# A diffusion mixer layer: recurrence gates as 64x64 fp32 quarter products instead of split 128x128 products

## Reference

```python
def lru_coeffs(xc, wa, ba, wx, bx, lam):
    xh = xc.reshape(B_, N, LRU_HEADS, LRU_HD)                # 8 heads of 64 channels
    r = sigmoid(einsum('bnhi,hij->bnhj', xh, wa).reshape(B_, N, W_LRU) + ba)
    i = sigmoid(einsum('bnhi,hij->bnhj', xh, wx).reshape(B_, N, W_LRU) + bx)
    log_a = (-LRU_C * r) * softplus(-lam)
    a = exp(log_a)
    b = sqrt(-expm1(2.0 * log_a)) * (i * xc)
    return a, b                                              # h_t = a_t * h_(t-1) + b_t, forwards and backwards
```

## Time and profile before

| what | value |
|---|---|
| median of 3 runs | 792.26 us (788.52 to 792.53) |
| the profiled execution | 792.91 us, span 790.7 us |
| mean granted TensorE clock | 0.971 of full speed |
| busy PE / PEld / DVE / ACT / POOL | 739.8 / 602.7 / 526.6 / 449.5 / 272.5 us |
| the projection's and output's matmuls (lines 1544 to 1546) in the chain that ended last | 57% of the span |

### The profile page before, as it was taken

How to read it: one execution, slowest core, us unless ns; L and a number is a source line. 1 busy time by engine, 2 the same in 40 slices (tenths; PEclk the granted TensorE clock), 3 DMA queues, 4 the chain that set the end, 5 groups by cost and what they waited for, 6 DMA issues and landing times.

```text
span 790.7 us, 9934 instructions
## 1 busy us (share of the span) xinstructions
PE 739.8 (94%) x3468; PEld 602.7 (76%) x3468; DVE 526.6 (67%) x811; ACT 449.5 (57%) x743; POOL 272.5 (34%) x321
## 2 busy tenths in 40 slices
PE   3886989999999999999998999899999999999997
PEld 1574767888888887888887877677787888888885
DVE  4377653757998798887995754776646665666522
ACT  4266643699786986787884982234535133534311
POOL 0122335243534274234423345233211134353421
PEclk9796989999999999999999999899999999999999
DMA  8997003334365355345444043254458667968531
GB/s 360 369 325 225 27 28 96 105 97 117 115 182 151 86 157 176 112 141 162 146 130 137 34 127 135 82 160 134 116 194 315 223 205 244 302 202 293 181 116 72
DMA packets 89218, 130.11 MB, mean 165 GB/s; under 512 B 22768, under 2 KB 54128, under 8 KB 87632
## 3 DMA queue, kind: packets, MB, share of 16 engines
q1 hardware_dynamic: 84800, 115.44, 45.1%
q0 software_dynamic: 4368, 14.03, 6.4%
HBM read 91.17 MB, written 38.27 MB: 164 GB/s over the span
## 4 chain that ended last, share of the span: by engine, by line
PE 59%; DVE 14%; issue 7%; ACT 7%; DMA 7%; POOL 4%; SPq 1%; DVEq 0%; ACTq 0%; POOLq 0%
PE bank L1544 19%; PE bank L1546 19%; PE bank L1545 19%; DMA wm<-in_w_mod 3%; DMA pv<-scratch_u 1%; DVE xg L1186 1%; DVE Qb L1301 1%; DVE xc L1129 1%; ACT fbuf L895 1%; DVE spl L1348 1%; POOL xTh L609 1%; ACT bank L878 1%; DVE xTl L1194 1%; DVE Ib L1291 1%; DVE gacc L1129 1%
## 5 line engine op out<-in xcount | busy, mean ns | idle before, releaser
L1544 PE MATMUL bank<-xTh,wh 128*128 128x512 f32 (+1 forms) x592 | 238.2, 402 | 7.2 <-DVE xTl L1194 4.4
L1546 PE MATMUL bank<-xTh,wl 128*128 128x512 f32 (+1 forms) x592 | 231.9, 392 | 0.0
L1545 PE MATMUL bank<-xTl,wh 128*128 128x512 f32 x576 | 227.2, 395 | 0.0
L1544 PEld LDWEIGHTS bank<-xTh,wh 128*128 128x128 f32 x592 | 113.8, 192 | 32.8 <-DVE xTl L1194 6.4
L1546 PEld LDWEIGHTS bank<-xTh,wl 128*128 128x128 f32 x592 | 113.3, 191 | 23.7
L1545 PEld LDWEIGHTS bank<-xTl,wh 128*128 128x128 f32 x576 | 110.2, 191 | 22.6 <-issue 1.2
L1544 PE MATMUL bank<-xTh 128*128 128x512 f32 (+1 forms) x272 | 104.2, 383 | 1.3 <-issue 0.8
L1546 PE MATMUL bank<-xTh,xTl 128*128 128x512 f32 x256 | 99.6, 389 | 0.0
L1545 PE MATMUL bank<-xTl,xTh 128*128 128x512 f32 x256 | 99.6, 389 | 0.0
L911 ACT ACTIVATE ustage<-bank 128x512 f32<-128x512 f32 x56 | 33.1, 592 | 93.0 <-PE bank L1546 76.3
L609 POOL TENSOR_SCALAR sph<-xc 128x512 fp32r<-128x512 f32 (+1 forms) x36 | 27.1, 769 | 121.1 <-PE bank L1546 68.4
(11 more groups left out here) (192 smaller groups left out, 1413.0 us busy)
## 6 DMA issues: line engine op xcount, KB each, us to landing
scratch_u<-ustage SPq DMA_DIRECT2D x72, 256.0 KB, 3.3
wraw<-in_w_in SPq DMA_DIRECT2D x18, 512.0 KB, 4.6
wm<-in_w_mod SPq DMA_DIRECT2D x8, 1024.0 KB, 14.4
xg<-in_x SPq DMA_DIRECT2D x16, 512.0 KB, 9.0
yb<-scratch_y SPq DMA_DIRECT2D x32, 256.0 KB, 3.6
gb<-scratch_u SPq DMA_DIRECT2D x32, 256.0 KB, 5.1
xres<-in_x SPq DMA_DIRECT2D x16, 512.0 KB, 4.7
out<-tout SPq DMA_DIRECT2D x15, 512.0 KB, 3.0
```

The source lines that it names most:

```text
L1544: mm(out, wh_, xh_, start=first, stop=False)
L1545: mm(out, wh_, xl_, start=False, stop=False)
L1546: return mm(out, wl_, xh_, start=False, stop=last)
```

## The change

The gates become plain fp32 matmuls on the raw operands. Each of the four 64x64 blocks of a direction is a matmul of its own on a quarter of the array: input rows 0-63 or 64-127, output partitions 0-63 or 64-127. The recurrence gate `gr` uses the two diagonal quarters, the input gate `gi_` the two crossed ones, so the halves of `gi_` come out exchanged, and ACT takes them over crosswise with two sigmoids of 64 partitions for each direction. The splits of `xc` and of the gate weights go, with `sph`, `spl`, `gwh`, `gwl`, their zeroing and their semaphores; `gwr` gets two buffers. The sigmoid of `gr` goes to a new SBUF buffer `rb`, which holds the Tanh too. PE waits for the convolved pieces themselves and for all six sigmoids of the step before. The high parts of the projection weights 5 to 15 and of all conv weights move from ACT to POOL: those that stood behind the sigmoids now stand ahead of `gated_input(q)`, the others ahead of `add_y(q)`. On DVE `conv(here + 4)` moves from behind the scans of s = 0 to behind `one_minus_a2` of s = 1. The buffers behind keep their addresses.

```diff
@@ SBUF
-        sph = a3.take("sph", [P, 2, CH], f32r)
-        spl = a3.take("spl", [P, 2, CH], f32r)
...
-        gwh = a3.take("gwh", [P, 4, P], f32r)
-        gwl = a3.take("gwl", [P, 4, P], f32r)
-        gwr = a3.take("gwr", [P, 4, 64])
+        gwr = a3.take("gwr", [P, 2, 4, 64])
+        rb = a3.take("rb", [P, 2, CH])
+        a3.off += 4 * (2 * CH + 2 * 4 * P - 4 * 64)
@@ helpers
+        ON_POOL = [w for w in range(5, len(W_JOBS)) if w_split_at(w) <= GATES_AFTER[-1]]
@@ gpsimd
-            g.memset(gwh[:].bitcast(f32), 0.0).then_inc(s_gz, 1)
-            g.memset(gwl[:].bitcast(f32), 0.0).then_inc(s_gz, 1)
...
             def load_gate_w(t):
-                if t:
-                    pool.wait_ge(s_gwl, 2 * t)
-                g.dma_start(gwr[:], gate_w[t]).then_inc(s_gw, 16)
+                if t >= 2:
+                    pool.wait_ge(s_pg, (NCH + 1) * (t - 1))
+                g.dma_start(gwr[:, t % 2], gate_w[t]).then_inc(s_gw[t % 2], 16)
...
-            def gate_w_hi(t):
...
-            def split(q):
...
                 for d, c in enumerate((f, b)):
-                    pool.wait_ge(s_sig, 4 * q + d + 3)
+                    pool.wait_ge(s_sig, 6 * q + 2 * d + 4)
...
+            def w_hi(w):
+                pool.wait_ge(s_wr[w % 2], 16 * (w // 2))
+                pool.wait_ge(s_pu, w_slot_free(w))
+                round_hi(W_JOBS[w][1][0], w_raw(w)).then_inc(s_whp, 1)
+
+            def conv_w_hi(j):
+                pool.wait_ge(s_cwr[j % 2], 16 * (j // 2 + 1))
+                if j >= 2:
+                    pool.wait_ge(s_pu, N_CU + CONV_AT[j - 2] + 1)
+                round_hi(cwh[:, j % 2], cwraw[:, j % 2]).then_inc(s_cwhi, 1)
+
+            done_w, done_cw = 5, 0
+
+            def weights_hi(upto):
+
+                nonlocal done_w, done_cw
+                while done_w - 5 < len(ON_POOL) and w_split_at(done_w) <= upto:
+                    w_hi(done_w)
+                    done_w += 1
+                while done_cw < N_CONV and CONV_AT[done_cw] - 4 <= upto:
+                    conv_w_hi(done_cw)
+                    done_cw += 1
...
-            gate_w_hi(0)
-            split(0)
...
-                if s == NCH and more:
-                    gate_w_hi(t + 1)
                 if s == 0:
                     load_v(here + 4)
-                if q + 1 < STEPS:
-                    split(q + 1)
...
+                if GATES_AFTER[q] + 1 in WEIGHTS_BEHIND_GATES:
+                    weights_hi(GATES_AFTER[q] + 1)
                 gated_input(q)
...
                 for j in convs_in_step(q, 4):
                     conv_z_hi(j)
+                weights_hi(min(STEP_END[q], GATES_AFTER[-1]))
                 add_y(q)
@@ scalar, sigmoids
                 for d in range(2):
-                    r = gr[d][:, 0:n]
-                    a.activation(r, r, ACT.Sigmoid, bias=par_col("lru_ba", 4 * d + t)).then_inc(s_sig, 1)
+                    a.activation(rb[:, d, 0:n], gr[d][:, 0:n], ACT.Sigmoid,
+                                 bias=par_col("lru_ba", 4 * d + t)).then_inc(s_sig, 1)
                 for d in range(2):
                     if q:
                         act.wait_ge(s_st, 2 * (q - 1) + d + 1)
-                    a.activation(Ib[:, d, 0:n], gi_[d][:, 0:n], ACT.Sigmoid,
-                                 bias=par_col("lru_bx", 4 * d + t)).then_inc(s_sig, 1)
+                    for h, other in ((slice(0, 64), slice(64, 128)), (slice(64, 128), slice(0, 64))):
+                        a.activation(Ib[h, d, 0:n], gi_[d][other, 0:n], ACT.Sigmoid,
+                                     bias=par_col("lru_bx", 4 * d + t)[h]).then_inc(s_sig, 1)
@@ scalar, decays
-                    r = gr[d][:, 0:n]
+                    r = rb[:, d, 0:n]
@@ scalar, the loop over the steps
-                if GATES_AFTER[q] + 1 in WEIGHTS_BEHIND_GATES:
-                    weights_side(GATES_AFTER[q] + 1)
@@ vector, one_minus_a2
-                    stt(Qb[:, d, 0:n], Qb[:, d, 0:n], 1.0, gr[d][:, 0:n], ALU.add, ALU.mult).then_inc(s_m2, 1)
+                    stt(Qb[:, d, 0:n], Qb[:, d, 0:n], 1.0, rb[:, d, 0:n], ALU.add, ALU.mult).then_inc(s_m2, 1)
@@ vector, the loop over the steps
-                if s == NCH and t + 1 < N_LRU:
-                    gate_w_lo(t + 1)
...
                 one_minus_a2(q)
-                if q + 1 < STEPS:
-                    split_lo(q + 1)
+                if s == 1:
+                    conv(here + 4)
...
                 if s == 0:
                     conv(here + 3)
-                    conv(here + 4)
@@ tensor, gates
                 if s == 0:
-                    pe.wait_ge(s_gwl, 2 * t + 2)
-                pe.wait_ge(s_sl, splits_before(q + 1))
+                    pe.wait_ge(s_gw[t % 2], 16 * (t // 2 + 1))
+                pe.wait_ge(s_cv, (NCH + 1) * t + LAST_PIECE[s] + 1)
                 if q:
-                    pe.wait_ge(s_sig, 4 * q)
-                    pe.wait_ge(s_m2, 2 * q)
-                for m in range(4):
-                    d = 0 if s == 0 else m // 2
-                    b = gi_[m // 2] if m % 2 else gr[m // 2]
-                    ins = mm3(b[:, 0:n], gwh[:, m, :], gwl[:, m, :], sph[:, d, 0:n], spl[:, d, 0:n], True, True)
+                    pe.wait_ge(s_sig, 6 * q)
+                w, top, low = gwr[:, t % 2], slice(0, 64), slice(64, 128)
+                for d, c in enumerate(step_chunks(s)):
+                    x = xc_piece(t, c)
+                    mm(gr[d][top, 0:n], w[top, 2 * d], x[top], start=True, stop=True)
+                    mm(gr[d][low, 0:n], w[low, 2 * d], x[low], start=True, stop=True)
+                    mm(gi_[d][low, 0:n], w[top, 2 * d + 1], x[top], start=True, stop=True)
+                    ins = mm(gi_[d][top, 0:n], w[low, 2 * d + 1], x[low], start=True, stop=True)
                 ins.then_inc(s_pg, 1)
```

More of the change, by code:

```diff
@@ L97, in convs_in_step @@
     return [g for g in range(N_CONV) if GATES_AFTER[q] <= CONV_AT[g] - lead < STEP_END[q]]
-def splits_before(q):
-    t, s = divmod(q, NCH + 1)
-    return (2 * NCH + 1) * t + (2 * s - 1 if s else 0)
 def mixer_kernel(nc, x, ctx, par, w_mod, b_gate, g_post, w_in, gate_w, pool_w, conv_dw, conf_pw, w_out,
@@ L283, in mixer_kernel @@
         s_wr, s_whi, s_wlo = [sem(f"w_raw_in{b}") for b in range(4)], sem("w_hi"), sem("w_lo")
+        s_whp = sem("w_hi_on_pool")
         s_pu, s_ev = sem("unit_done"), sem("unit_evacuated")
         s_us = [sem(f"u_stored{b}") for b in range(U_SLOTS)]
-        s_gz, s_gw, s_gwh, s_gwl = sem("gatew_zeroed"), sem("gatew_in"), sem("gatew_hi"), sem("gatew_lo")
+        s_gw = [sem(f"gatew_in{b}") for b in range(2)]
         s_v, s_cv = [sem(f"v_in{b}") for b in range(2)], sem("convolved")
-        s_sh, s_sl, s_pg, s_sig = sem("split_hi"), sem("split_lo"), sem("gates_done"), sem("sigmoids")
+        s_pg, s_sig = sem("gates_done"), sem("sigmoids")
         s_aq, s_exp, s_m2, s_rt = sem("a_and_q"), sem("tanhs"), sem("one_minus_a2"), sem("roots")
@@ L931, in decays @@
                     kc = 4 * d + t
-                    act.wait_ge(s_sig, 4 * q + d + 1)
+                    act.wait_ge(s_sig, 6 * q + d + 1)
                     if s == 0 and t or s == 4:
                         act.wait_ge(s_ya, 4 * t if s == 0 else 4 * t + 2)
-                    r = gr[d][:, 0:n]
+                    r = rb[:, d, 0:n]
                     a.activation(Ab[:, d, 0:n], r, ACT.Exp, scale=kn[:, kc:kc + 1]).then_inc(s_aq, 1)
@@ L952, in conv_sigmoid @@
                 a.activation(x_, x_, ACT.Sigmoid).then_inc(s_cgs, 1)
[L954 to L959, removed]
             first, second = range(0, KD // 2), range(KD // 2, KD)
@@ L1007, in weights_side @@
             def weights_side(n):
-                for w in range(5, len(W_JOBS)):
+                for w in range(5 + len(ON_POOL), len(W_JOBS)):
                     if n == w_split_at(w):
                         w_hi(w)
-                for j in range(N_CONV):
-                    if n == CONV_AT[j] - 4:
-                        conv_w_hi(j)
             def unit_side(n):
-                if n not in WEIGHTS_BEHIND_GATES:
-                    weights_side(n)
+                weights_side(n)
                 evac(N_CU + n)
@@ L1156, in w_lo @@
             def w_lo(w):
-                dve.wait_ge(s_whi, w + 1)
+                if w in ON_POOL:
+                    dve.wait_ge(s_whp, w - 4)
+                else:
+                    dve.wait_ge(s_whi, w + 1 if w < 5 else w + 1 - len(ON_POOL))
                 h, l = W_JOBS[w][1]
@@ L1248, in _ @@
             lo_group(NCH)
-            def gate_w_lo(t):
-                for i, h in enumerate((slice(0, 64), slice(64, 128))):
-                    dve.wait_ge(s_gwh, 2 * t + i + 1)
-                    v.tensor_tensor(out=gwl[h, :, h], in0=gwr[h], in1=gwh[h, :, h].bitcast(f32),
-                                    op=ALU.subtract).then_inc(s_gwl, 1)
             def conv(p):
@@ L1339, in conv_w_lo @@
```

(10 more changed lines are left out.)

## The result

The changed kernel takes 804.8 us (median of 4), the kernel before 792.0: a ratio of 1.017 (95% interval 1.013 to 1.021), so it is slower by a small amount that is clear of the noise. One of the four executions took 1038.3 us at a mean granted clock of 0.655; the ratio goes by the other three (803.7 to 805.0 us). Forecast was 781, with 776 to 798 as the range. The profiled execution took 803.7 us, with a span of 801.6.

A forecast was written before the change was run, and what follows sets the result against it. TensorE was taken to bound the middle (busy 315.8 of 320.7 us). Gates -11.8, moved conv +1.4, old waits -1.4 and -0.8, behind the middle +1.2 gave -11.4 us: 781 us, range 776 to 798.

The forecast's parts named there:

- The gate matmuls: Gate steps of the middle: quarters run four abreast, 2.1 us a full step instead of 2.78; 11.8 us saved.
- (b): Gate steps: quarters run only two abreast, 3.8 us a full step, +18.8 instead of -11.8, giving 811 us; chance 0.11.
- (c): Gate steps: no overlap, 872 us, or 0.3 us more for each switch of shape, 793 us; chance 0.06.
- ACT: Steps of the middle: two added half-height sigmoids make the chain 1.15 us longer; costed at nothing, 1 us at worst.
- the wait behind the middle: Behind the last gates: their chain is 1.15 us longer, so +1.2 us, first at the wait for `ustage`.
- Level totals: ACT in the middle: loses weight writes of 11.9 + 11.7 us, gains sigmoids of 21.4 us, so its total stays level.
- The moved conv: Gates of step s = 2: PE waits 1.4 us for the conv in the first tile, zero in the others.
- The weights on GpSimd: High parts on GpSimd: some 34 us, near the load it loses; the slots are free early, so costed at nothing.
- The two old waits: PE's waits for conv units at 298.50 (1.57 us) and 420.23 (3.14 us): shrink by 1.4 and 0.8 us.
- My own sign of being wrong: Prediction wrong if PE waits add over 8 us in the middle, or a gate step holds PE over 2.4 us.
- Rival (a): DVE's new order takes the saving back through waits at tile 2 and conv units and lost clock: 789 us; chance 0.13.

The follow-up runs named there:

- e8: Changed kernel with one whole input-gate sigmoid per direction instead of two halves and three staging buffers instead of two (not a valid layer): 777.1 us, 0.981.
- e1: Changed kernel with one 128-partition input-gate sigmoid per direction instead of two of 64 (output not the reference's): 786.8 us, 0.995.
- e5: Kernel before with only its input gate's sigmoid split into two uncrossed halves of 64 partitions: 806.8 us, 1.022.
- e4: Changed kernel with three staging buffers for evacuated units instead of two: 788.9 us, 0.9955.
- e7: Changed kernel, still two staging buffers, with the first evacuation of a step moved ahead of the roots: 790.3 us, 1.002.
- e2: Changed kernel with the fifth conv piece back behind the scans of the context step: 804.5 us, 1.016.
- e10: Kernel before with only the high parts of the middle's weights moved to GpSimd: 796.3 us, 1.008.
- e3: Changed kernel with the high parts of the 27 weights back on ACT, in their old places: 812.1 us, 1.026.
- e6: Changed kernel with the recurrence gate and the tanh back in PSUM, PE waiting for `one_minus_a2` again: 800.5 us, 1.014.
- e9: Changed kernel with three staging buffers and every sigmoid of the middle as a tanh, GpSimd adding 1 to the input gate: 789.8 us, 1.0005.

## Why the prediction was wrong, step by step

- **The gate matmuls: right.** 2.08 us a step for 2.1, four abreast, bank pairs of different rows included. Rivals (b) and (c) did not occur, and e8 shows 11.4 us of the 11.8.
- **ACT: this step failed.** I wrote that ACT "did 12.0 in their 13.7 and will need 13.2" against PE's 13.0, "so I cost that at nothing, 1 us at worst". In these steps the need was 13.9 without the scan's wait and 14.6 with it. The added half costs 0.77 us, not 0.575 (2.81 us for four against 1.27 for two whole ones), and six activations with operands in SBUF start 0.61 us apart where PSUM had 0.57. But even by my own 13.2 ACT was over PE's 13.0, and I excused it with PE's four banks. The four banks let PE go on with its projection units; they do nothing for the chain sigmoid, glu, z, conv unit, nor for the wait behind the middle, where there are two banks. And "only three such steps follow each other" left out the steps with a conv unit: there ACT works 14.9 us and PE takes 14.8, so these steps win no lateness back. e1 prices the term in the changed kernel: without the halves its ratio falls by 2.2% (1.017 to 0.995). e5 prices it in the kernel before: the halves alone are +2.2%.
- **The reaction of a late ACT: left out.** I never asked what ACT waits for when it is late. It waits less for PE (16 us instead of 34) and so meets its own stores, 40 us of waits instead of 18. One more buffer returns 17 us (e4), one moved evacuation 12 (e7), both by the ratios.
- **Level totals.** ACT's work was to stay equal (it grew by 11 us), but the weights that left stood in few steps, the halves came in every one. A sum over 320 us hid that. On DVE 28 us were to go, and 22 went: the product with `rb` in SBUF instead of PSUM takes 845 ns instead of 684 at 512 columns and 1032 instead of 420 at 256, 10 us in all, which I had not priced. GpSimd's high parts of the weights took 24.6 us, where I had some 34.
- **The moved conv: near in tile 0, wrong in two others, and worth nothing.** 1.77 us were measured for 1.4 in tile 0, and 1.01 and 1.13 in tiles 1 and 2, where I took zero. Taking it back changed nothing (e2), because ACT was late anyway.
- **The weights on GpSimd at nothing: not right either way.** Alone they cost the kernel before 0.8% (e10); in the changed kernel the relief of ACT is worth more than that, and they gain 0.9% (e3).
- **The two old waits were to shrink**; they grew from 1.6 and 3.1 to conv-unit waits of 5.1, 5.1, 3.3 and 2.7 us. With ACT relieved twice (e8) two "issue" waits are left in the middle, 3.9 us together. The wait behind the middle was to grow by 1.2 and grew by 6.0. My own sign of being wrong, over 8 us more of waits in the middle, came with 15 us more of idle time.
- **Balance of the two profiled executions** (+10.9 us of span): the first gate step came 4.1 us earlier, mostly because the clock stayed at 1.00 behind the wait at 108 us, where it was 0.50 in the earlier trace rows. This is not the change's: from 110.4 to 117 us it was 1.00 in e5, which has nothing of the change there, and 0.50 in e3 and e6, which start as the changed kernel does. The middle is 8.2 longer (PE busy 7.0 less, idle 15.2 more), all behind it 6.8. Of the 11.4 us of matmul time that e8 shows saved, PE gave 4.4 back (busy 308.8 against 304.4), with a granted clock of 0.97 in the middle against 0.99. Behind the wait of 5.09 us the changed kernel's stretch reads:

```profile
299.10:303.00 3.90, 3.86 (x17) 3.79 (x18) 3.83 (x5) 1.65 (x4) 1.62 (x1) 0.50 0.54 168
```

- Rival (a) named the place (conv units, clock) but not the cause, and ended at 789. None of the rivals made ACT the bound.

## What to carry to other kernels

Work that an engine off the path takes over must be held against its step, not against its total: when it needs more than the bound engine's step (here 13.9 to 14.6 us of 13.0, and 14.9 of 14.8), it is the bound until a step gives it slack. Ask then what the late engine will run into (here two staging buffers), since that sets the size of the loss. A layout that needs two activations more a step can cost more than the matmuls it saves. Price an activation by the distance of starts, and do not expect half the time for half the partitions.

## What the runs showed of the hardware

- Activations of 64 x 512 elements from PSUM to SBUF lasted 684 ns, as long as those of 128 x 512 (694). They started 0.70 us apart, crossed or not (e5), and whole ones 0.575. Why they do not overlap stays open.
- Four fp32 matmuls on the four 64x64 quarters ran at once, at 0.43 us for each pass of 512 columns at the clock of 1.00; two pairs of them wrote one bank each, from different rows to different partitions.
- Reading from SBUF instead of PSUM cost ACT 15 to 36 ns an activation (708 and 716 ns against 672 and 693; the tanh, with 36, also wrote to SBUF instead of PSUM).
- An exponential of 128 x 512 in SBUF took 804 ns with a scale and a bias per partition (e9) and 716 with the scale alone (after).
- DVE's scalar_tensor_tensor of 128 x 512 took 845 ns on the average with both inputs in SBUF (after) and 684 and 686 with one in PSUM (before, e6). How much of that is GpSimd's work beside it is not shown.
- With more work on GpSimd, DVE's operations took longer: 980 to 1285 ns for an operand split when only the weights moved to GpSimd (e10), and 2.33 to 6.05 us for three operations of a conv beside GpSimd's work (e4).
